# ScalarE takes over the product of the one-hots with the high parts of the gates, one token at a time

## The chip, the core and the metric

The kernel runs on one core of a Trainium2 chip. The metric is the device time of one execution in microseconds (us). TensorE is PE in the profile (PEld its weight loads), VectorE is DVE, ScalarE is ACT, GpSimd is POOL, SyncE is SP.

## The reference, cut to what matters

The program is two transformer blocks over 512 tokens. The part at stake is the product-key expert layer of the first one (`peer_ffn`): 8 heads choose 16 of 128 x 128 experts each, so every token has 128 picks, and each pick is a pair (a, b) of key numbers with a gate.

```python
idx = jnp.take_along_axis(cand_i, best_p, axis=-1)      # a * 128 + b
gate = jax.nn.softmax(best_s, axis=-1)
act = jax.nn.gelu(jnp.einsum('nd,nhkd->nhk', xi, u[idx]), approximate=False)
return jnp.einsum('nhk,nhkd->nd', (gate * act), v[idx])
```

## The kernel before

For 384 of the 512 tokens (`DT`) the kernel computes all 16384 experts densely. For each token it needs a 128 x 128 matrix of gates: entry (b, a) is the sum of the gates of the picks with that pair. This matrix is a product of two one-hot matrices over the 128 picks, which lie on the 128 partitions: `left` has a one where the key equals the pick's a, `right` where it equals the pick's b, and `right` times the gate is the other factor. The gate is split into a high and a low bf16 part, so the product is taken twice and summed in PSUM. The remaining 128 tokens (`ROW_TILE`) take another way: for each of their picks GpSimd gathers one expert row of 4 KB per partition from `u` or `v` (512 KB for one pick of all 128 tokens) into one of four row slots, and VectorE multiplies or adds it (`VectorProgram.rows`).

The stage at stake is `gate_matrices`. It has 48 steps (`HOT_STEPS`) of 8 tokens (`OC`). The one-hots lie as [group of 4 tokens, key, token], so that the four tokens of a group (`OI`) are neighbours in memory, and one token's 128 keys lie 8 bytes apart. In a step of the kernel before:

- **VectorE** writes `left` (L1981), `right` (L1984), `right` times the gates' high parts (L1986) and `right` times the low parts (L1987), each 128 x 1024 bf16. Then it uses the gathered rows that are due, 1.5 per step on average (`ROWS_HOT`; L1827 dots with `u`, L1840 sums with `v`), and, once in 8 steps, in the fourth of them, subtracts the low part of a weight block (L1851, 128 x 4096).
- **TensorE** waits for the step's one-hots, does 16 matmuls of 128 x 128 (L802: 8 tokens, two parts), and after every odd step a *fill tile*: 24 matmuls of 384 columns for one tile of expert activations (`fill`, L456 to L458). In the kernel before, both matmuls of a token load the same `left` as weights and stream one of the gated ones.
- **ScalarE** copies the two PSUM banks of a step into `gate_matrices` (L1348, with a strided write: four tokens go side by side for each key), takes the fill tile through Gelu (L1304), and once in 8 steps, before the Gelu of the second one, writes the high part of a weight block (L1060, 128 x 4096).
- **SyncE** stores 2 MB of gate matrices every 4 steps, loads 2 MB of weights every 8 steps (once the low part that frees the stage buffer is done; its next entries stand behind that wait), and spills each fill tile (192 KB).
- **GpSimd** issues the row gathers, each when the row four before it has been used.

The one-hots are double buffered over steps (`v = n % 2`), except `right`, which has one buffer. VectorE may begin step n when TensorE has done step n-2. All engines run orders written out by hand; semaphores join them, and each engine works strictly down its own list. "A period" below is 8 steps: 4 fill tiles, 12 gathered rows, one weight block, two stores. The stage is 6 periods. It is followed by fill tiles alone (`LAST_FILL`) and then the expert sums, in which TensorE has work without a break.

Of the kernel before, what the change touches and what calls it, by code (L numbers as in the profile page):

```python
# [14 lines left out]
P = 128  # L15
D = 1024
# [60 lines left out]
class Signals:  # L77


    def __init__(self, nc, reached):  # L80
# [51 lines left out]
        self.row_act = self.new("row_experts_activated")  # L132

# [14 lines left out]
        self.hot = self.new("one_hots_ready")  # L148
# [39 lines left out]
class Layout:  # L188


    def __init__(self, nc, n_columns):
# [54 lines left out]
        self.left, self.right = hot("one_hot_a", one_hots, BF16), hot("one_hot_b", one_hots[:1] + one_hots[2:], BF16)  # L246
        self.gated = [hot(f"gated_one_hot_b_{part}", one_hots, BF16) for part in range(2)]
# [13 lines left out]
        self.row_sum = Map(nc, m.at)("row_sum", [P, D])  # L261
# [168 lines left out]
class TensorProgram:  # L430
# [361 lines left out]
    def gate_matrices(self):  # L792
        nc, s, k, m = self.nc, self.s, self.k, self.m
        for n in range(DT // OC):
            v = n % 2
            nc.tensor.wait_ge(*s.hot.at(n))
            for q in range(OC // 4):
                event = ("gate_mats", n, q)
                i = self.take(event, (s.act_out, event))
                for x in range(4):  # L800
                    for part in range(2):
                        ins = nc.tensor.matmul(k.psum[:, i, NK * x:NK * (x + 1)], m.left[:, v, q, :, x],  # L802
                                               m.gated[part][:, v, q, :, x], start=part == 0, stop=part == 1)
                ins.then_inc(*s.gate_mats.up(n, q))
# [241 lines left out]
class ScalarProgram:  # L1046
# [290 lines left out]

    def gate_matrices(self):
        nc, s, k, m = self.nc, self.s, self.k, self.m
        for n in range(HOT_STEPS):  # L1340
# [177 lines left out]
class VectorProgram:  # L1518
# [374 lines left out]
    def route(self):  # L1893
# [5 lines left out]
        for o, t in enumerate(ROUTE_TILES):  # L1899
# [61 lines left out]
            nc.vector.wait_ge(*s.copied.at("picks", t))  # L1961
            nc.vector.tensor_tensor(m.pick_b[:, 3, at], k.psum[:, k.bank_of["picks", t], 2 * P:3 * P],
                                    m.pick_b[:, 2, at], ALU.subtract).then_inc(*s.routed.up("split", t))

    def gate_matrices(self):
# [8 lines left out]
        for n in range(HOT_STEPS):  # L1974
            v, tokens = n % 2, slice(OC * n, OC * (n + 1))
            number_a, number_b, gate_high, gate_low = (
                m.pick_b[:, x, tokens].rearrange("p (c n) -> p c n", n=OI).unsqueeze(2).to_broadcast(hots)
                for x in range(4))
            if n >= 2:
                nc.vector.wait_ge(*s.gate_mats.at(n - 2, OC // 4 - 1))  # L1980
            nc.vector.tensor_tensor(m.left[:, v], iota, number_a, ALU.is_equal).then_inc(*s.step.up())  # L1981
            if n >= 1:
                nc.vector.wait_ge(*s.hot.at(n - 1))
            nc.vector.tensor_tensor(m.right[:, :, :, :], iota, number_b, ALU.is_equal).then_inc(*s.step.up())  # L1984
            nc.vector.wait_ge(*s.step.now())
            nc.vector.tensor_tensor(m.gated[0][:, v], m.right[:, :, :, :], gate_high, ALU.mult).then_inc(*s.step.up())  # L1986
            nc.vector.tensor_tensor(m.gated[1][:, v], m.right[:, :, :, :], gate_low, ALU.mult).then_inc(*s.hot.up(n))  # L1987
# [493 lines left out]
```

## Time and profile before

| | |
|---|---|
| median of 3 runs | 2749.22 us (2747.74 to 2750.6) |
| the profiled execution, its own time | 2750.3 us |
| its span | 2749.0 us |
| busy: PE, DVE, ACT, POOL | 2468.8, 1567.8, 964.3, 889.2 us |
| gate-matrix stage, first one-hot to the Gelu of its last fill tile | 1177.3 to 1435.4 us of the span |

Busy times are sums over the whole span; what a change in one stage is worth has to be read from that stage. The granted TensorE clock is in tenths of full speed: 1.0 is 2.4 GHz, 0.5 is 1.2 GHz. Matmuls overlap, so two starts are nearer than one matmul is long; the same holds to a smaller degree for ScalarE and VectorE.

### The profile page before, as it was taken

How to read it: one execution, taken by the hardware profiler on the slowest of the kernel's cores; microseconds unless marked ns; L12 is line 12 of the kernel's file. 1: busy time of each engine (PE TensorE's matmuls, PEld its weight loads, DVE VectorE, ACT ScalarE, POOL GpSimd, SP SyncE). 2: the span in 40 equal slices, each digit the busy share in tenths (PEclk: the TensorE clock that was granted, in tenths of full speed). 3: DMA queues.
4: the chain of work that ended last, by engine and by line, in shares of the span. 5: the costliest groups of instructions: out<-in, count | busy, mean ns of one | idle time of the engine just before them, and what ended most of it. 6: DMA issues, size and time to landing. Idle time of an engine off the chain costs nothing.

```text
span 2749.0 us, 32835 instructions
## 1 busy us (share of the span) xinstructions
PE 2468.8 (90%) x13363; PEld 1442.8 (52%) x13363; DVE 1567.8 (57%) x2616; ACT 964.3 (35%) x1122; POOL 889.2 (32%) x686
## 2 busy tenths in 40 slices
PE   6997679997879997968789999999979988899998
PEld 4455446653445554555565566666534466344443
DVE  2036452213289999998986888886455375333102
ACT  3116542313233333344444333333242343334310
POOL 3332252432114143334432333331116100354540
PEclk8998766889989999988889999999999998999999
DMA  4121111231159686778899999998412100123310
GB/s 167 62 93 62 63 62 62 92 123 55 54 172 327 231 316 214 280 266 307 297 342 327 382 389 382 385 376 297 153 46 92 51 28 8 62 94 121 123 62 31
DMA packets 194503, 484.78 MB, mean 176 GB/s; under 512 B 10741, under 2 KB 93731, under 8 KB 188336
## 3 DMA queue, kind: packets, MB, share of 16 engines
q1 hardware_dynamic: 154624, 334.65, 34.8%
q0 software_dynamic: 39728, 148.03, 14.3%
q8 instruction: 106, 1.74, 0.3%
q14 instruction: 45, 0.37, 0.0%
HBM read 430.21 MB, written 52.43 MB: 176 GB/s over the span
## 4 chain that ended last, share of the span: by engine, by line
PE 63%; DVE 21%; DMA 7%; ACT 4%; issue 2%; POOL 2%; SPq 0%; ACTq 0%; DVEq 0%; POOLq 0%
PE psum L456 16%; PE psum L457 16%; PE psum L458 16%; DMA rows_b<-u_rows_dram,row_index 4%; DVE weight_low L1851 3%; PE psum L707 3%; POOL weight_low L2153 2%; PE psum L689 2%; PE psum L514 2%; DMA rows_b<-peer_v_dram,row_index 2%; DVE row_sum L1840 1%; PE psum L941 1%; DVE picks L1943 1%; DVE rows_b L1827 1%; PE psum L601 1%
## 5 line engine op out<-in xcount | busy, mean ns | idle before, releaser
L456 PE MATMUL psum<-x_high,weight_high 128*128 128x384 bf16 (+3 forms) x1856 | 652.6, 352 | 67.2 <-DVE weight_low L1851 29.6
L2153 POOL TENSOR_TENSOR weight_low<-weight_stage,weight_high 128x512 bf16<-128x512 f32 (+1 forms) x373 | 463.9, 1281 | 740.7 <-ACT weight_high L1060 740.7
L457 PE MATMUL psum<-x_low,weight_high 128*128 128x384 bf16 (+3 forms) x1856 | 651.8, 351 | 0.0
L458 PE MATMUL psum<-x_high,weight_low 128*128 128x384 bf16 (+3 forms) x1856 | 650.4, 350 | 0.0
L1060 ACT ACTIVATE weight_high<-weight_stage 128x4096 bf16<-128x4096 f32 (+2 forms) x112 | 399.2, 3566 | 343.0 <-PE psum L458 310.4
L456 PE MATMUL psum<-hidden_high,weight_high 128*128 128x384 bf16 x1024 | 333.8, 326 | 1.0 <-DVE hidden_low L2006 0.9
L458 PE MATMUL psum<-hidden_high,weight_low 128*128 128x384 bf16 x1024 | 333.8, 326 | 0.0
L457 PE MATMUL psum<-hidden_low,weight_high 128*128 128x384 bf16 x1024 | 333.8, 326 | 0.0
L456 PEld LDWEIGHTS psum<-x_high,weight_high 128*128 128x128 bf16 (+1 forms) x1856 | 186.2, 100 | 236.9 <-issue 37.3
L1851 DVE TENSOR_TENSOR weight_low<-weight_stage,weight_high 128x4096 bf16<-128x4096 f32 x64 | 282.8, 4419 | 29.0 <-ACT weight_high L1060 29.0
L458 PEld LDWEIGHTS psum<-x_high,weight_low 128*128 128x128 bf16 (+1 forms) x1856 | 186.3, 100 | 159.3 <-issue 14.7
L457 PEld LDWEIGHTS psum<-x_low,weight_high 128*128 128x128 bf16 (+1 forms) x1856 | 186.0, 100 | 149.2 <-issue 10.6
L2256 POOL DMA_INDIRECT rows_a<-u_rows_dram,row_index x64 | 88.7, 1386 | 355.6 <-DVE rows_a L1827 265.7
L1304 ACT ACTIVATE norm_value<-psum 128x384 f32<-128x384 f32 x128 | 62.8, 491 | 354.0 <-PE psum L458 185.7
L2256 POOL DMA_INDIRECT rows_b<-u_rows_dram,row_index x64 | 96.6, 1510 | 218.5 <-DVE rows_b L1827 217.0
L802 PE MATMUL psum<-gated_one_hot_b,one_hot_a 128*128 128x128 bf16 x768 | 97.7, 297 | 52.8 <-DVE gated_one_hot_b L1987 52.7
L2256 POOL DMA_INDIRECT rows_b<-peer_v_dram,row_index x64 | 102.8, 1607 | 117.6 <-DVE row_sum L1840 101.3
L456 PEld LDWEIGHTS psum<-hidden_high,weight_high 128*128 128x128 bf16 x1024 | 100.2, 98 | 67.6 <-issue 1.7
L458 PEld LDWEIGHTS psum<-hidden_high,weight_low 128*128 128x128 bf16 x1024 | 100.2, 98 | 66.2
L457 PEld LDWEIGHTS psum<-hidden_low,weight_high 128*128 128x128 bf16 x1024 | 100.2, 98 | 65.5
L2256 POOL DMA_INDIRECT rows_a<-peer_v_dram,row_index x64 | 96.7, 1510 | 84.1 <-DVE row_sum L1840 64.1
L802 PEld LDWEIGHTS psum<-gated_one_hot_b,one_hot_a 128*128 128x128 bf16 x768 | 85.9, 120 | 65.2 <-DVE gated_one_hot_b L1987 63.1
(321 smaller groups left out, 3551.5 us busy)
## 6 DMA issues: line engine op xcount, KB each, us to landing
weight_stage<-peer_u_dram SPq DMA_DIRECT2D x32, 2048.0 KB
weight_stage<-peer_v_dram SPq DMA_DIRECT2D x32, 2048.0 KB
weight_stage<-mlp_w_dram SPq DMA_DIRECT2D x16, 2048.0 KB
weight_stage<-ada_w_dram SPq DMA_DIRECT2D x12, 2048.0 KB
act_dram<-norm_value SPq DMA_DIRECT2D x128, 192.0 KB
gate_dram<-gate_matrices SPq DMA_DIRECT2D x12, 2048.0 KB, 17.1
gates<-gate_dram SPq DMA_DIRECT2D x32, 768.0 KB, 16.5
expert_act<-act_dram SPq DMA_DIRECT2D x32, 768.0 KB
```

What stands on the lines that cost most here:

```text
L456: self.nc.tensor.matmul(out, left[0], right[0], start=first, stop=False)
L457: self.nc.tensor.matmul(out, left[0], right[1], start=False, stop=False)
L458: return self.nc.tensor.matmul(out, left[1], right[0], start=False, stop=last)
L514: ins = nc.tensor.matmul(k.bank(i, hi - lo), self.m.ones[:, :], buffers.square[:, t % 4, lo:hi], start=t == 0, stop=t == KT - 1, skip_grou ...
L689: ins = nc.tensor.matmul(k.psum[0:JT, j + ni * i // HT, ni * i % HT:ni * i % HT + ni], ka[rows, a, JT * jt:JT * (jt + 1)], qa[rows, a, i0: ...
L707: ins = nc.tensor.matmul(k.psum[:, 6 + half, i0 - HT * half:i0 - HT * half + ni], m.gv[:, jt, P * head:P * (head + 1)], weight[n % 3][:, n ...
L802: ins = nc.tensor.matmul(k.psum[:, i, NK * x:NK * (x + 1)], m.left[:, v, q, :, x], m.gated[part][:, v, q, :, x], start=part == 0, stop=par ...
L1060: nc.scalar.activation(k.block_view(m.w_high, n % SPLITS, n), k.block_view(m.w_stage, n % STAGES, n), ACT.Copy).then_inc(*s.w_high.up(n))
L1304: nc.scalar.activation(m.norm2.value[:, tile % 4, 0:DT], k.tile_bank(event, DT), ACT.Gelu).then_inc(*s.activated.up(*event))
L1851: nc.vector.tensor_tensor(k.block_view(m.w_low, n % SPLITS, n), k.block_view(m.w_stage, n % STAGES, n), k.block_view(m.w_high, n % SPLITS, ...
L2153: ins = nc.gpsimd.tensor_tensor(m.w_low[:, n % SPLITS, at], m.w_stage[:, n % STAGES, at], m.w_high[:, n % SPLITS, at], ALU.subtract)
L2256: nc.gpsimd.indirect_dma_start(m.rows[i % ROW_SLOTS], None, v if layer else u, index).then_inc(*s.in_rows[i % ROW_SLOTS].up(i))
```

## The change

ScalarE multiplies `left` (the one-hots of a, no longer those of b) with the gates' high parts, one instruction per token: 128 partitions x 128 keys, read 8 bytes apart, written as one contiguous row into a new tile `gated_high`, with the token's column of a new f32 tile `gate_high` as the scale (a [128, 1] operand). VectorE keeps three 128 x 1024 operations: `left`, `right`, and `left` times the low parts. `right` gets a second buffer. TensorE now loads the gated one-hots as weights (the high ones contiguous, the low ones strided as before) and streams `right`. In `ScalarProgram.gate_matrices` the products of step n come ahead of the copies of step n-1. In `route`, VectorE copies each tile's gates once more into f32 (3 copies of 128 x 128).

```diff
+        self.hot_gated = self.new("one_hots_gated")
...
-        self.left, self.right = hot("one_hot_a", one_hots, BF16), hot("one_hot_b", one_hots[:1] + one_hots[2:], BF16)
-        self.gated = [hot(f"gated_one_hot_b_{part}", one_hots, BF16) for part in range(2)]
+        self.left, self.right = hot("one_hot_a", one_hots, BF16), hot("one_hot_b", one_hots, BF16)
+        self.gated_high = hot("one_hot_a_gated_high", [P, 2, OC, NK], BF16)
+        self.gated_low = hot("one_hot_a_gated_low", one_hots, BF16)
...
             nc.tensor.wait_ge(*s.hot.at(n))
+            nc.tensor.wait_ge(*s.hot_gated.at(n, OC - 1))
...
-                    for part in range(2):
-                        ins = nc.tensor.matmul(k.psum[:, i, NK * x:NK * (x + 1)], m.left[:, v, q, :, x],
-                                               m.gated[part][:, v, q, :, x], start=part == 0, stop=part == 1)
+                    for part, left in enumerate((m.gated_high[:, v, 4 * q + x, :], m.gated_low[:, v, q, :, x])):
+                        ins = nc.tensor.matmul(k.psum[:, i, NK * x:NK * (x + 1)], left, m.right[:, v, q, :, x],
+                                               start=part == 0, stop=part == 1)
...
+    def gate_hots(self, n):
+        nc.scalar.wait_ge(*s.hot_made.at(n))
+        if n >= 2:
+            nc.scalar.wait_ge(*s.gate_mats.at(n - 2, OC // 4 - 1))
+        for x in range(OC):
+            at = OC * n + x
+            nc.scalar.activation(m.gated_high[:, v, x, :], m.left[:, v, x // OI, :, x % OI], ACT.Copy,
+                                 scale=m.gate_high[:, at:at + 1]).then_inc(*s.hot_gated.up(n, x))
...
-        for n in range(HOT_STEPS):
+        for step in range(HOT_STEPS + 1):
+            if step < HOT_STEPS:
+                self.gate_hots(step)
+            if step == 0:
+                continue
+            n = step - 1
...
+            nc.vector.tensor_copy(m.gate_high[:, at], m.pick_b[:, 2, at]).then_inc(*step.up())
...
             if n >= 2:
                 nc.vector.wait_ge(*s.gate_mats.at(n - 2, OC // 4 - 1))
-            nc.vector.tensor_tensor(m.left[:, v], iota, number_a, ALU.is_equal).then_inc(*s.step.up())
-            if n >= 1:
-                nc.vector.wait_ge(*s.hot.at(n - 1))
-            nc.vector.tensor_tensor(m.right[:, :, :, :], iota, number_b, ALU.is_equal).then_inc(*s.step.up())
-            nc.vector.wait_ge(*s.step.now())
-            nc.vector.tensor_tensor(m.gated[0][:, v], m.right[:, :, :, :], gate_high, ALU.mult).then_inc(*s.step.up())
-            nc.vector.tensor_tensor(m.gated[1][:, v], m.right[:, :, :, :], gate_low, ALU.mult).then_inc(*s.hot.up(n))
+                nc.vector.wait_ge(*s.hot_gated.at(n - 2, OC - 1))
+            nc.vector.tensor_tensor(m.left[:, v], iota, number_a, ALU.is_equal).then_inc(*s.hot_made.up(n))
+            nc.vector.tensor_tensor(m.right[:, v], iota, number_b, ALU.is_equal).then_inc(*s.step.up())
+            nc.vector.wait_ge(*s.hot_made.at(n))
+            nc.vector.tensor_tensor(m.gated_low[:, v], m.left[:, v], gate_low, ALU.mult).then_inc(*s.hot.up(n))
```

ScalarE's list in the middle of the stage before: the copies of two steps stand together (`gate_matrices`), then a fill tile's Gelu (`norm_value`), once in 8 steps with the weight block's high part (`weight_high`) ahead of it.

```order
L1348 ACTIVATE gate_matrices<-psum 128x4x128 x4
L1304 ACTIVATE norm_value<-psum 128x384
L1348 ACTIVATE gate_matrices<-psum 128x4x128 x4
L1060 ACTIVATE weight_high<-weight_stage 128x4096
L1304 ACTIVATE norm_value<-psum 128x384
```

The same list after the change, two steps with a fill tile and a weight block between them; `one_hot_a_gated_high` are the eight products of a step.

```order
L1351 ACTIVATE one_hot_a_gated_high<-one_hot_a,gates_t_high 128x128 x8
L1369 ACTIVATE gate_matrices<-psum 128x4x128 x2
L1064 ACTIVATE weight_high<-weight_stage 128x4096
L1308 ACTIVATE norm_value<-psum 128x384
L1351 ACTIVATE one_hot_a_gated_high<-one_hot_a,gates_t_high 128x128 x8
L1369 ACTIVATE gate_matrices<-psum 128x4x128 x2
L1351 ACTIVATE one_hot_a_gated_high<-one_hot_a,gates_t_high 128x128 x8
L1369 ACTIVATE gate_matrices<-psum 128x4x128 x2
L1308 ACTIVATE norm_value<-psum 128x384
```

The products of step n+2 stand behind the Gelu of the fill tile that follows step n (n odd), and those of step n+3 behind the copies of step n+1.

VectorE's list, one step before, and one after; `rows_a` and `row_sum` are uses of gathered rows, `in_rows_0` and `in_rows_1` the gathers they wait for.

```order
L1827 SCALAR_TENSOR_TENSOR rows_a,modulation_rows<-rows_a,normed_rows 128x1024 [waits in_rows_0]
L1981 TENSOR_TENSOR one_hot_a<-iota_bf_135,picks_t_bf_107 128x1024 [waits gate_matrices_ready]
L1984 TENSOR_TENSOR one_hot_b<-iota_bf_135,picks_t_bf_107 128x1024 [waits one_hots_ready]
L1986 TENSOR_TENSOR gated_one_hot_b_124<-one_hot_b,picks_t_bf_107 128x1024 [waits vector_steps]
L1987 TENSOR_TENSOR gated_one_hot_b_125<-one_hot_b,picks_t_bf_107 128x1024
L1840 SCALAR_TENSOR_TENSOR row_sum<-rows_a,modulation_rows,row_sum 128x1024 [waits rows_used,in_rows_1]
```

```order
L1848 SCALAR_TENSOR_TENSOR rows_a,modulation_rows<-rows_a,normed_rows 128x1024 [waits in_rows_0]
L2004 TENSOR_TENSOR one_hot_a<-iota_bf_136,picks_t_bf_107 128x1024 [waits one_hots_gated,gate_matrices_ready]
L2005 TENSOR_TENSOR one_hot_b<-iota_bf_136,picks_t_bf_107 128x1024
L2007 TENSOR_TENSOR one_hot_a_gated_low<-one_hot_a,picks_t_bf_107 128x1024 [waits one_hots_made]
L1861 SCALAR_TENSOR_TENSOR row_sum<-rows_a,modulation_rows,row_sum 128x1024 [waits rows_used,in_rows_1]
```

One of four 128 x 1024 operations is gone from each step, and the wait of the second product for the one just before it has become a wait for the one two before.

## Rows read from the trace of the kernel before

**Rows 1.** Windows of the stage, one period, and what follows (columns in the first line).
```profile
core 0: us, PE busy (x) PEld busy (x) DVE busy (x) ACT busy (x) POOL busy (x), PEclk, DMA share, GB/s
1281.40:1324.54 43.14, 33.93 (x226) 24.56 (x225) 38.67 (x52) 21.33 (x22) 16.95 (x13) 0.82 0.85 311
1435.00:1500.00 65.00, 64.94 (x400) 38.93 (x399) 38.35 (x37) 27.39 (x26) 13.69 (x11) 1.00 0.91 325
```

**Rows 2.** Waits in 1177 to 1433: who for whom, us in total, times, longest.
```profile
PE psum L802 <- DVE gated_one_hot_b L1987: 52.7, 29, 4.1
DVE rows_b L1827 <- DMA rows_b<-u_rows_dram,row_index: 21.0, 11, 3.9
DVE row_sum L1840 <- DMA rows_b<-peer_v_dram,row_index: 2.6, 5, 0.6
```

**Rows 3.** VectorE's timeline, one step: start us, us, operation.
```profile
1319.59 0.69 DVE L1981 TENSOR_TENSOR one_hot_a<-iota_bf,picks_t_bf 128x1024 bf16<-128x1024 bf16 x1
1320.19 0.69 DVE L1984 TENSOR_TENSOR one_hot_b<-iota_bf,picks_t_bf 128x1024 bf16<-128x1024 bf16 x1
1320.91 0.69 DVE L1986 TENSOR_TENSOR gated_one_hot_b<-one_hot_b,picks_t_bf 128x1024 bf16<-128x1024 bf16 x1
1321.52 0.68 DVE L1987 TENSOR_TENSOR gated_one_hot_b<-one_hot_b,picks_t_bf 128x1024 bf16<-128x1024 bf16 x1
1322.12 1.22 DVE L1827 SCALAR_TENSOR_TENSOR rows_a<-rows_a,normed_rows 128x1024 f32<-128x1024 f32 x1
```

**Rows 4.** Chain of waits, 1281 to 1330: two gathers from issue to landing (start us, us).
```profile
1289.67 13.40 DMA rows_b<-u_rows_dram,row_index
...
1304.85 9.83 DMA rows_b<-u_rows_dram,row_index
```

**Rows 5.** TensorE's timeline at one short pause; [idle before <-releaser] at the end.
```profile
1404.62 2.05 PE L802 MATMUL psum<-gated_one_hot_b,one_hot_a 128*128 128x128 bf16 x16
1407.20 2.06 PE L802 MATMUL psum<-gated_one_hot_b,one_hot_a 128*128 128x128 bf16 x16 [0.53 <-DVE gated_one_hot_b L1987]
1409.08 0.50 PE L456 MATMUL psum<-x_high,weight_high 128*128 128x384 bf16 x1
...
1411.61 0.44 PE L458 MATMUL psum<-x_high,weight_low 128*128 128x384 bf16 x1
1411.89 0.33 PE L456 MATMUL psum<-x_high,weight_high 128*128 128x384 bf16 x1
1412.06 0.33 PE L457 MATMUL psum<-x_low,weight_high 128*128 128x384 bf16 x1
```

**Rows 6.** TensorE's weight loads at full clock: 32 strided ones, one contiguous one.
```profile
1298.55 3.82 PEld L802 LDWEIGHTS psum<-gated_one_hot_b,one_hot_a 128*128 128x128 bf16 x32
...
1302.83 0.10 PEld L456 LDWEIGHTS psum<-x_high,weight_high 128*128 128x128 bf16 x1
```

**Rows 7.** ScalarE's timeline, Gelu, weight block, copies of two steps.
```profile
1363.90 3.95 ACT L1348 ACTIVATE gate_matrices<-psum 128x512 f32<-128x512 f32 x4 [0.45 <-PE psum L802]
...
1435.49 0.49 ACT L1304 ACTIVATE norm_value<-psum 128x384 f32<-128x384 f32 x1 [2.85 <-PE psum L458]
1435.88 3.61 ACT L1060 ACTIVATE weight_high<-weight_stage 128x4096 bf16<-128x4096 f32 x1
```

**Rows 8.** ScalarE's timeline, runs of one form without and with a [128, 1] operand.
```profile
2038.13 1.74 ACT L1109 ACTIVATE norm_square<-na_q 128x256 f32<-128x256 f32 x5
...
2045.31 1.31 ACT L1120 ACTIVATE ctx_high<-norm_value,modulation 128x256 bf16<-128x256 f32 x3 [2.34 <-DVE norm_value L1575]
```

**Rows 9.** Groups by form on ScalarE: busy us, mean ns of one | idle before.
```profile
L1348 ACT ACTIVATE gate_matrices<-psum 128x512 f32<-128x512 f32 x96 | 95.9, 1088 | 66.6 <-PE psum L802 65.6 <-issue 0.9
...
L1320 ACT ACTIVATE scores<-psum 128x512 f32<-128x512 f32 x16 | 9.6, 597 | 22.8 <-PE psum L776 22.8
...
L1120 ACT ACTIVATE ctx_high<-norm_value,modulation 128x256 bf16<-128x256 f32 x8 | 3.8, 504 | 3.8 <-DVE norm_value L1575 3.8
...
L1109 ACT ACTIVATE norm_square<-na_q 128x256 f32<-128x256 f32 x8 | 2.8, 406 | 0.3 <-issue 0.3
```

More of the change, by code:

```diff
@@ L147, in __init__ @@
         self.routed = self.new("experts_chosen")
-        self.hot = self.new("one_hots_ready")
+        self.hot_made, self.hot = self.new("one_hots_made"), self.new("one_hots_ready")
         self.gated = self.new("hidden_gated")
@@ L260, in __init__ @@
             self.mod_rows[:, PICKS * x:PICKS * (x + 1)] for x in range(4))
-        self.row_sum = Map(nc, m.at)("row_sum", [P, D])
+        behind = Map(nc, m.at)
+        self.row_sum, self.gate_high = behind("row_sum", [P, D]), behind("gates_t_high", [P, DT])
         self.keys = m("sub_keys", [P, 2 * PH, NK])
@@ L1336, in route @@
             self.row_experts(ROWS_ROUTE[ROUTE_TILES.index(chosen)])
+    def gate_hots(self, n):
+        nc, s, m = self.nc, self.s, self.m
+        v = n % 2
+        nc.scalar.wait_ge(*s.hot_made.at(n))
[5 more added lines that the diff above has]
+                                 scale=m.gate_high[:, at:at + 1]).then_inc(*s.hot_gated.up(n, x))
     def gate_matrices(self):
         nc, s, k, m = self.nc, self.s, self.k, self.m
-        for n in range(HOT_STEPS):
+        for step in range(HOT_STEPS + 1):
[4 more added lines that the diff above has]
+            n = step - 1
             chunk, part = n // (TC // OC), n % (TC // OC)
@@ L1975, in gate_matrices @@
             v, tokens = n % 2, slice(OC * n, OC * (n + 1))
-            number_a, number_b, gate_high, gate_low = (
+            number_a, number_b, gate_low = (
                 m.pick_b[:, x, tokens].rearrange("p (c n) -> p c n", n=OI).unsqueeze(2).to_broadcast(hots)
-                for x in range(4))
+                for x in (0, 1, 3))
             if n >= 2:
                 nc.vector.wait_ge(*s.gate_mats.at(n - 2, OC // 4 - 1))
-            nc.vector.tensor_tensor(m.left[:, v], iota, number_a, ALU.is_equal).then_inc(*s.step.up())
-            if n >= 1:
-                nc.vector.wait_ge(*s.hot.at(n - 1))
-            nc.vector.tensor_tensor(m.right[:, :, :, :], iota, number_b, ALU.is_equal).then_inc(*s.step.up())
-            nc.vector.wait_ge(*s.step.now())
-            nc.vector.tensor_tensor(m.gated[0][:, v], m.right[:, :, :, :], gate_high, ALU.mult).then_inc(*s.step.up())
-            nc.vector.tensor_tensor(m.gated[1][:, v], m.right[:, :, :, :], gate_low, ALU.mult).then_inc(*s.hot.up(n))
+                nc.vector.wait_ge(*s.hot_gated.at(n - 2, OC - 1))
[3 more added lines that the diff above has]
+            nc.vector.tensor_tensor(m.gated_low[:, v], m.left[:, v], gate_low, ALU.mult).then_inc(*s.hot.up(n))
             self.rows(ROWS_HOT[n])
```

## The prediction

> **What bounds the kernel now.** First the windows. From 1435 us on TensorE works without a break at full clock [rows 1], and the expert sums behind that are its work too, so what the gate-matrix stage gains or loses in its 258.1 us goes whole into the time. In a period of the stage (43.14 us, 8 steps) TensorE is busy 33.93 us at a mean clock of 0.82, ScalarE 21.33, VectorE 38.67 [rows 1]. The waits say who leads: TensorE waits 52.7 us for VectorE's last product, VectorE only for gathered rows, 21.0 + 2.6 us [rows 2], which is 3.9 us a period. So VectorE's list sets the pace, with the gathers as its second term.
>
> **VectorE's share of the change.** One step's four operations take from 1319.59 to 1322.12, 2.53 us, of which 0.72 lie between the second and third start and 0.60 to 0.61 between the others: the third waits for the second [rows 3]. After the change three remain, and the product waits for the operation two before, so 3 x 0.60 = 1.80 us. That is 0.73 less a step, 5.8 us a period. The gathers give part of it back. A slot is refilled when VectorE has used it, and a refill issued into the stores and weight loads takes 13.40 and 9.83 us to land [rows 4], whatever VectorE does meanwhile. Four slots at 1.5 rows a step are 2.7 steps, which cover 2.7 x 0.73 = 1.9 us less than before; two waits a period make 3.9 us. VectorE with its gathers would then need 43.0 - 5.8 + 3.9 = 41.1 us a period (43.0 is 258.1/6). This is the floor that the other engines have to stay under.
>
> **ScalarE's share.** A product of 128 elements with a [128, 1] scale is not in the trace. Its neighbours are there: 256 elements take 406 ns without such an operand and 504 with one [rows 9], and back to back three of the latter end after 1.31 us, so 0.403 us from start to start [rows 8]. Five of the former end after 1.74 us, 0.334 apart. The length part: from 256 to 512 elements of the plain form (406 to about 597 ns by the PSUM copies, [rows 9]) is 0.75 ns an element, from the 1.74 us run's 256 elements to the 4096 of the weight block (3.61 us, [rows 7]) 0.83. With 0.83, half the length takes 0.107 us off: 0.296 us from start to start, 0.40 for one alone. Eight are 2.37 us of ScalarE, and the last one is done 7 x 0.296 + 0.40 + 0.06 = 2.53 us after the first begins. I bound the pitch below by 0.25 (the operand costs nothing in a stream) and above by 0.42: the copies into `gate_matrices` write with a stride and take 1088 ns where contiguous ones take 597 [rows 9], 0.96 ns an element more, and the products read with a stride of 8 bytes. I take 0.296, since all but the stride is measured, and the doubled row has a stride of 128 bytes, on the write side. By the doubled row the sum would be 24 us above mine (the third rival). SBUF — State Buffer in the Trainium skill (the note on 16-byte cachelines) says that a strided read keeps full bandwidth while two accesses fall in one 16-byte line; 8 bytes is just that, and by this rule the stride costs nothing. No row here shows a strided read on ScalarE.
>
> A period's ScalarE work becomes 64 x 0.296 = 18.9 for the products, 16 x 0.95 = 15.2 for the copies (four end after 3.95, [rows 7]), 3.5 for the weight block and 4 x 0.39 for Gelu [rows 7]: 39.2 us where it had 21.3. It now nearly fills the period, and its order matters.
>
> **The new loop.** The products of step n+2 stand behind the Gelu of the fill tile after step n, and that fill tile stands behind the matmuls of step n on TensorE. So from one Gelu to the next, two steps on, one chain runs: Gelu 0.39; eight products 2.53; 16 matmuls; the fill tile; Gelu. The 16 matmuls took 1407.20 to 1409.08, 1.88 us [rows 5]. Their weight loads go at 3.82/32 = 0.119 us strided and 0.10 contiguous [rows 6]; half become contiguous, so 1.88 - 8 x 0.019 = 1.73. The fill tile is 23 x 0.1625 (64.94 us for 400 matmuls, [rows 1]) + 0.37 = 4.11 us at full clock. The clock will not be full. In the loop TensorE finishes the even step's matmuls (their products are ready) and then waits about 1 us for the odd step's, and a pause of only 0.53 us in just this place put the nine matmuls after it on the 1.2 GHz level, 0.32 apart instead of 0.16 [rows 5]. Nine are 1.4 us; I take 1.0, since the phase will vary. Sum: 0.39 + 2.53 + 1.73 + 4.11 + 1.0 = 9.8, times four 39.0.
>
> Once a period the weight block comes in. Then ScalarE, after the odd step's products, still has 1.9 (copies), 2.4 (products), 1.9 (copies), 3.5 = 9.7 us before Gelu, while TensorE needs 0.05 + 1.73 + 4.11 + 1.0 = 6.9: 2.8 us over. Without the block 6.2 is under 6.9. VectorE's low part makes one `left` a period late; I put 0.4 for it, between nothing and 1. A period: 39.0 + 2.8 + 0.4 = 42.2 us, above VectorE's 41.1 and 0.8 below today's 43.0. Six periods: -4.8.
>
> **Small terms.** The first matmul waits for `left` and eight products, 0.69 + 2.53, instead of 2.65: +0.5. Three f32 copies of 128 x 128 in `route`: only the last is ahead of the stage, +0.2. The second `right` buffer changes nothing, as VectorE was never stopped by the first. TensorE's count, DMA bytes and all tables of ScalarE stay. Sum -4.8 + 0.7 = -4.1, so the profiled 2750.3 becomes 2746; against the median (2749.2) that is 3 us less. A measurement of this kernel can tell about 0.2% (5.5 us) from no change, so my likeliest case is no measurable change.
>
> **Rivals.**
> *The loop stays at full clock.* If the shorter, regular pauses leave the clock up, the loop is 8.8 x 4 + 3.8 + 0.4 = 39.4, and VectorE with its gathers decides at 41.1: 6 x 1.9 = -11, 2739. For it: TensorE's idle share falls; against: the 0.53 us pause [rows 5].
> *VectorE's whole gain arrives.* If in addition the gathers land earlier, because the stores follow the copies and shift, the waits stay at 3.9 and the period is the loop's 39.4 or so: -22, 2728. Against: bytes per us rise while the DMA share is already 0.85 [rows 1].
> *ScalarE's products become the bound* (the other side). ScalarE's list is then full. Its pair of steps is 0.39 + 16 p + 3.8 with p the pitch; four of them and the block are 43.0 at p = 0.355, and with the loop's wait for TensorE the turn comes earlier, at about 0.31, only 15 ns above my figure. At 0.35 the period is some 44.5 and the kernel 2759; at 0.42, ScalarE alone needs 26.9 + 20.3 = 47.2 and the kernel is at 2775. For it: the doubled copies [rows 9]; TensorE stands, VectorE idles. ScalarE: Activation LUTs in the Trainium skill (rules for kernel authors) says to multiply on VectorE, not ScalarE. Row by row it would speak for this rival: 8 x 0.296 = 2.37 us replace 0.73. It leaves open that the engine giving is the bound and the one taking idles.
> That the change doesn't do what it says I rule out: the products are in ScalarE's list and gone from VectorE's.
>
> **How the numbers follow.** The loop with clock dips, 0.40 (2740 to 2752; a quarter of it under -5.5); the loop at full clock 0.20; the whole gain 0.10; products moderately dear (pitch 0.32 to 0.36) 0.16; products doubled 0.14. Faster: 0.20 + 0.10 + 0.10 = 0.40. Within 0.2%: 0.28 of the first and a little of the fourth, 0.30. Slower: 0.30. The range leaves out the far parts of the second and last rival: 2728 to 2771.
>
> **What would show it.** Right: the products at 0.40 us alone and 0.29 to 0.30 apart, ScalarE busy over 85% of the stage; TensorE waiting once per two steps, now for ScalarE's products, 0.8 to 1.5 us; a longer such wait once in 8 steps, where the weight block stands; fill tiles still partly on the 1.2 GHz level; VectorE's own four operations down to 1.80 us, and its idle time grown, for rows or for TensorE's step n-2. The step that is weakest is the clock in the loop, then the stride. Wrong: TensorE waiting for VectorE's low product as now (the gathers lead, not the loop), or products over 0.31 apart.

## The result, and the profile after

| | before | after |
|---|---|---|
| median | 2748.11 us (20 runs) | 2754.12 us (20 runs) |
| ratio | | 1.0028 [1.0019, 1.0036] |
| the profiled execution, its own time | 2750.3 us | 2753.76 us |
| its span, mean TensorE clock | 2749.0 us, 0.916 | 2752.5 us, 0.914 |
| stage: first one-hot to the Gelu of its last fill tile | 1177.32 to 1435.49 us | 1178.89 to 1443.27 us |

The changed kernel is slower by 0.28%, 6.0 us by the medians and 7.7 by the ratio. A time of 2746 had been predicted, with no measurable change as the likeliest case. In the profiled runs the stage takes 6.2 us more, close to the 6.0 us of the medians, and its last Gelu comes 7.8 us later; 1.4 us of that offset stand in the trace at 113 us already, far ahead of anything that the change touches. Behind the last Gelu the profiled execution of after is 4.3 us shorter (1309.2 against 1313.5 us), although nothing differs there. In all thirteen traces of this case that part takes 1308.2 to 1313.5 us, and two executions of one kernel (e2) are 3.6 us apart in it. So the stages of two traces can be compared, their whole times only by the medians.

The page of after, busy time by engine over the whole span:

```profile
PE 2477.7 (90%) x13295; PEld 1448.3 (53%) x13363; DVE 1536.9 (56%) x2571; ACT 1071.2 (39%) x1506; POOL 873.2 (32%) x686
```

The stage as one window (columns as in [rows 1]):

```profile
1178.90:1440.00 261.10, 218.27 (x1328) 152.55 (x1329) 201.46 (x260) 234.79 (x511) 87.34 (x72) 0.80 0.85 308
```

VectorE is busy 201 of 261 us, no longer nearly all of the time; ScalarE 235 of 261, 90%. The clock of the stage stays at 0.80. The work has moved as planned. Who waits, in 1177 to 1440 (who for whom, us in total, times, longest), against [rows 2]:

```profile
PE psum L806 <- issue: 44.4, 25, 4.9
ACT norm_value L1308 <- PE psum L461: 21.6, 16, 1.8
DVE one_hot_a L2004 <- PE psum L806: 16.3, 12, 3.0
DVE row_sum L1861 <- DMA rows_b<-peer_v_dram,row_index: 15.6, 6, 3.1
DVE weight_low L1872 <- ACT weight_high L1064: 13.5, 6, 3.2
ACT one_hot_a_gated_high L1351 <- DVE one_hot_a L2004: 5.0, 9, 1.6
DVE rows_b L1848 <- DMA rows_b<-u_rows_dram,row_index: 4.7, 4, 2.4
DVE row_sum L1861 <- DMA rows_a<-peer_v_dram,row_index: 3.0, 2, 2.1
```

TensorE waits 44.4 us, but no longer for VectorE. "issue" names no releaser; the pauses lie where the odd steps' products are missing, and in the kernels below that have a matmul in that pause, the same wait is put down to `one_hot_a_gated_high`. ScalarE waits for TensorE's fill tiles 16 times, and VectorE now waits for TensorE, for ScalarE and for rows. So two engines wait for each other in turn. ScalarE's timeline (start, us, engine, line, operation, form, count, [idle before]) shows one turn of it:

```profile
1303.09 0.49 ACT L1308 ACTIVATE norm_value<-psum 128x384 f32<-128x384 f32 x1 [1.72 <-PE psum L461]
1303.48 2.50 ACT L1351 ACTIVATE one_hot_a_gated_high<-one_hot_a,gates_t_high 128x128 bf16<-128x128 bf16 x8
1305.88 2.02 ACT L1369 ACTIVATE gate_matrices<-psum 128x512 f32<-128x512 f32 x2
1307.69 2.46 ACT L1351 ACTIVATE one_hot_a_gated_high<-one_hot_a,gates_t_high 128x128 bf16<-128x128 bf16 x8
1310.05 1.99 ACT L1369 ACTIVATE gate_matrices<-psum 128x512 f32<-128x512 f32 x2
1313.53 0.49 ACT L1308 ACTIVATE norm_value<-psum 128x384 f32<-128x384 f32 x1 [1.49 <-PE psum L461]
...
1322.23 3.62 ACT L1064 ACTIVATE weight_high<-weight_stage 128x4096 bf16<-128x4096 f32 x1
1325.75 0.47 ACT L1308 ACTIVATE norm_value<-psum 128x384 f32<-128x384 f32 x1
```

and TensorE's timeline shows the other half of the turn; answers to [rows 5]:

```profile
1304.63 0.29 PE L806 MATMUL psum<-one_hot_b,one_hot_a_gated_low 128*128 128x128 bf16 x1
1306.08 0.28 PE L806 MATMUL psum<-one_hot_b,one_hot_a_gated_high 128*128 128x128 bf16 x1 [1.15 <-issue]
1306.17 0.30 PE L806 MATMUL psum<-one_hot_b,one_hot_a_gated_low 128*128 128x128 bf16 x1
...
1307.92 0.50 PE L459 MATMUL psum<-x_high,weight_high 128*128 128x384 bf16 x1
1308.22 0.53 PE L460 MATMUL psum<-x_low,weight_high 128*128 128x384 bf16 x1
...
1311.05 0.33 PE L460 MATMUL psum<-x_low,weight_high 128*128 128x384 bf16 x1
1311.21 0.33 PE L461 MATMUL psum<-x_high,weight_low 128*128 128x384 bf16 x1
```

The even step's matmuls are done, TensorE pauses 1.15 us for the odd step's products, and ten of the fill tile's matmuls start about 0.32 us apart (1.2 GHz) before the rest start 0.16 apart (2.4 GHz). In the stage's 24 fill tiles 218 matmuls start at that wide distance, where it was 111 before. They are called slow matmuls from here on.

From Gelu to Gelu (1303.09 to 1313.53) the turn takes 10.44 us: Gelu 0.39, products until the first matmul behind them 2.60 (1303.48 to 1306.08), 16 matmuls 1.84 (to 1307.92), fill tile to Gelu 5.61. The four turns from 1281.46 to 1325.75 take 11.00, 10.63, 10.44 and, with the weight block, 12.22: a period of 44.3 us, where 42.2 had been predicted and 43.0 was the old one. Of the five whole periods between the Gelus behind a weight block, three are like that (44.25, 44.29, 44.34); the first takes 42.8 and the last 41.4. The stage as a whole takes 264.4 us, a sixth of it 44.1.

### The profile page after: what moved, and what is told of

It reads as the page before. It is cut to its first block, busy times and chain, and to the rows that moved or that the text cites. A ratio compares the mean times of both kernels' runs of the same rounds, so it can differ in the third digit from the quotient of the medians.

```text
span 2752.5 us, 33198 instructions
## 1 busy us (share of the span) xinstructions
PE 2477.7 (90%) x13295; PEld 1448.3 (53%) x13363; DVE 1536.9 (56%) x2571; ACT 1071.2 (39%) x1506; POOL 873.2 (32%) x686
## 4 chain that ended last, share of the span: by engine, by line
PE 70%; DVE 17%; ACT 4%; issue 3%; DMA 3%; POOL 2%; SPq 0%; ACTq 0%; DVEq 0%; POOLq 0%
PE psum L459 17%; PE psum L460 17%; PE psum L461 17%; PE psum L806 3%; PE psum L710 3%; DVE weight_low L1872 3%; POOL weight_low L2173 2%; PE psum L692 2%; PE psum L517 2%; DMA rows_b<-peer_v_dram,row_index 2%; DVE picks L1964 1%; PE psum L945 1%; PE psum L604 1%; ACT weight_high L1064 1%; DVE norm_value L1596 1%
## 5 line engine op out<-in xcount | busy, mean ns | idle before, releaser
L460 PE MATMUL psum<-x_low,weight_high 128*128 128x384 bf16 (+3 forms) x1843 | 654.7, 355 | 21.0 <-DVE x_low L1605 14.8
L459 PEld LDWEIGHTS psum<-x_high,weight_high 128*128 128x128 bf16 (+1 forms) x1856 | 188.0, 101 | 240.5 <-issue 43.6
L806 PE MATMUL psum<-one_hot_b,one_hot_a_gated_high 128*128 128x128 bf16 x384 | 92.3, 295 | 44.4 <-issue 44.4
L1351 ACT ACTIVATE one_hot_a_gated_high<-one_hot_a,gates_t_high 128x128 bf16<-128x128 bf16 x384 | 119.4, 398 | 5.0 <-DVE one_hot_a L2004 5.0
L2276 POOL DMA_INDIRECT rows_a<-peer_v_dram,row_index x64 | 81.4, 1272 | 83.3 <-DVE row_sum L1861 64.6
```

Of the source, the lines that this page charges most:

```text
L459: self.nc.tensor.matmul(out, left[0], right[0], start=first, stop=False)
L460: self.nc.tensor.matmul(out, left[0], right[1], start=False, stop=False)
L806: ins = nc.tensor.matmul(k.psum[:, i, NK * x:NK * (x + 1)], left, m.right[:, v, q, :, x], start=part == 0, stop=part == 1)
L1351: nc.scalar.activation(m.gated_high[:, v, x, :], m.left[:, v, x // OI, :, x % OI], ACT.Copy, scale=m.gate_high[:, at:at + 1]).then_inc(*s. ...
L2276: nc.gpsimd.indirect_dma_start(m.rows[i % ROW_SLOTS], None, v if layer else u, index).then_inc(*s.in_rows[i % ROW_SLOTS].up(i))
```

## Experiments

Theory A: the loop of ScalarE and TensorE sets the period, and its fill tiles run partly at 1.2 GHz because of the pause in the loop itself. The rivals: VectorE or the gathers set the period; the clock does not matter; the products' price matters more than their place. All ratios are to the kernel before on the same chip. The diffs of e4 are against the kernel before, the others against the changed kernel unless said.

### e1: products ahead of the Gelu

```diff
-        for step in range(HOT_STEPS + 1):
-            if step < HOT_STEPS:
-                self.gate_hots(step)
-            if step == 0:
-                continue
-            n = step - 1
+        for n in range(2):
+            self.gate_hots(n)
+        for n in range(HOT_STEPS):
...
+            if n + 2 < HOT_STEPS:
+                self.gate_hots(n + 2)
```

> The changed kernel with one thing moved on ScalarE: the eight products of step n+2 stand right behind the copies of step n, ahead of the weight block and the Gelu of the fill tile, so they no longer wait for the end of that fill tile. ScalarE's work is the same. Theory A (the closed loop Gelu, products, matmuls, fill tile, Gelu sets the period of 44.3 us): the loop is open, the pauses of 1.13 and 3.1 us ahead of the odd steps shrink or go, the period falls to 41 to 42.6 us, where VectorE with its gathers and ScalarE's list meet, and the kernel to 2735 to 2744. Rival B (ScalarE's amount of work is the bound): nothing moves by more than 3 us, about 2754. Rival C (VectorE with the gathers still leads): also about 2754, with VectorE never waiting for TensorE.

Measured: 2749.84 us (12 runs), ratio 1.0009 [1.0000, 1.0019]; about 4 us under the changed kernel. Theory A had promised 2735 to 2744, so it gets the direction and misses the size. Its waits, 1177 to 1440:

```profile
ACT one_hot_a_gated_high L1351 <- DVE one_hot_a L2003: 25.9, 13, 2.9
DVE row_sum L1860 <- DMA rows_b<-peer_v_dram,row_index: 17.6, 6, 4.3
DVE weight_low L1871 <- ACT weight_high L1064: 17.6, 6, 3.7
```

ScalarE hardly waits for the fill tiles any more (2.3 us, once, instead of 21.6), so the loop is open, and the slow matmuls fall from 218 to 78. In its place two waits across VectorE grow: ScalarE's weight block now stands behind one more row of products, VectorE's low part waits longer for it (17.6 us instead of 13.5), and ScalarE's products wait longer for VectorE's one-hots (25.9 us instead of 5.0). VectorE's waits for rows grow too, from 23.3 to 39.7 us. The mean of four periods is 42.6 us (fill tiles from 1254.13 to 1424.63); the same four of the changed kernel take 43.6 (1242.03 to 1416.31). ScalarE's list alone would need 39.2 by the prediction's sum.

### e2: matmuls in the pause

TensorE does 384-column matmuls of no use into the bank that the step writes next, ahead of its wait for the odd step's one-hots: 7, and 20 in the step whose products follow the weight block. They end about where the products do, so they should take no time of their own.

```diff
+            first = self.take(("gate_mats", n, 0), (s.act_out, ("gate_mats", n, 0)))
+            for _ in range(0 if n % 2 == 0 or n < 3 else 20 if n % 8 == 3 else 7):
+                nc.tensor.matmul(k.psum[:, first, 0:DT], m.x_high[:, 0, 0:P], m.x_high[:, 1, 0:DT], start=True, stop=True)
```

> The changed kernel with 7 extra matmuls of 384 columns (20 once in 8 steps, ahead of the step after the weight block) on TensorE in its pause ahead of each odd step's one-hots, into the PSUM bank that the step then overwrites. They only keep TensorE busy while it waits. Theory A with the clock term: the nine or so matmuls a fill tile that run at the 1.2 GHz level (218 in the stage, 0.16 us each) go to full clock, the loop loses about 1.4 us a pair of steps, and the period falls from 44.3 to 41 or 42 us, where VectorE with its gathers takes over: 2735 to 2742. Rival (the clock is a side effect, the period is ScalarE's work or the gathers'): 2752 to 2756, fill tiles at full clock or not.

It was measured a second time, beside e9 and e10:

> The kernel of e2_paused_matmuls once more (7 extra matmuls ahead of odd steps, 20 in the step of the weight block), as the neighbour of the next two on the same chip. Both theories: a ratio to the kernel before of 0.997 to 0.9995, time 2740 to 2745.

Measured: 2742.81 us (12 runs), ratio 0.9984 [0.9975, 0.9993], and the second time 2742.88 us (11 runs), 0.9984 [0.9975, 0.9993]. It is 11 us faster than the changed kernel, by added work alone, and faster than the kernel before; theory A's range ended 0.8 us below it. Slow matmuls: 47 in the first profiled run, 22 in the second, instead of 218. The stage's window has the clock at 0.95:

```profile
1178.90:1440.00 261.10, 247.08 (x1660) 177.12 (x1660) 202.29 (x258) 238.49 (x510) 95.33 (x72) 0.95 0.85 316
```

Its Gelus (ScalarE's timeline) give the turn at full clock:

```profile
1358.37 0.46 ACT L1311 ACTIVATE norm_value<-psum 128x384 f32<-128x384 f32 x1
1368.92 0.49 ACT L1311 ACTIVATE norm_value<-psum 128x384 f32<-128x384 f32 x1 [1.01 <-PE psum L461]
1377.93 0.49 ACT L1311 ACTIVATE norm_value<-psum 128x384 f32<-128x384 f32 x1
1386.95 0.49 ACT L1311 ACTIVATE norm_value<-psum 128x384 f32<-128x384 f32 x1
```

9.01 and 9.02 us; where a pause of 1.16 us was left over, behind the weight block, ten matmuls are slow and the turn takes 10.55. The price of the clock in the loop is thus 1.5 us for ten slow matmuls. Not every turn is that short (the 18 without the weight block take 9.71 us on average): the mean period is 41.6 us (four from 1237.62 to 1404.07), and the waits name VectorE's side:

```profile
DVE row_sum L1864 <- DMA rows_a<-peer_v_dram,row_index: 17.3, 8, 2.8
DVE row_sum L1864 <- DMA rows_b<-peer_v_dram,row_index: 13.4, 6, 2.7
DVE rows_b L1851 <- DMA rows_b<-u_rows_dram,row_index: 8.8, 6, 2.3
ACT one_hot_a_gated_high L1354 <- DVE one_hot_a L2007: 11.1, 12, 2.5
```

With the loop nearly at full clock, the waits for rows rise to 39.5 us, 6.6 a period, from 23.6 [rows 2] and 23.3 in the changed kernel.

### e3: no low product

VectorE's low product is left out, and TensorE takes the plain one-hots in its place, so the output has ones in the place of the gates' low parts.

```diff
-                    for part, left in enumerate((m.gated_high[:, v, 4 * q + x, :], m.gated_low[:, v, q, :, x])):
+                    for part, left in enumerate((m.gated_high[:, v, 4 * q + x, :], m.left[:, v, q, :, x])):
...
-            nc.vector.tensor_tensor(m.gated_low[:, v], m.left[:, v], gate_low, ALU.mult).then_inc(*s.hot.up(n))
```

> The changed kernel without VectorE's product with the low parts: TensorE takes the plain one-hots of a as the second part, so the low parts of the gates are left out of the computation (ones in their place) and VectorE has 0.6 us less in each step. Theory A (the loop over ScalarE and TensorE sets the period, VectorE idles): within 2 us of the changed kernel, 2752 to 2756. Rival C (VectorE with the gathers sets it): up to 8 times 0.6 us a period less, given back in part by the gathers, 2735 to 2745.

Measured: 2753.5 us (10 runs), ratio 1.0024 [1.0014, 1.0035], with 219 slow matmuls. VectorE's 48 x 0.6 us = 29 us of work are gone and the time stays that of the changed kernel. VectorE waits that much more: 36.1 us for TensorE instead of 16.3, 28.1 for rows instead of 23.3, and 17.6 for the weight block instead of 13.5.

```profile
DVE one_hot_a L2004 <- PE psum L806: 36.1, 26, 3.7
```

That rules VectorE's list out as the bound of the changed kernel, as theory A had it (2752 to 2756).

### e4: the same matmuls in the kernel before

```diff
+            first = self.take(("gate_mats", n, 0), (s.act_out, ("gate_mats", n, 0)))
+            for _ in range(0 if n < 3 else 8 if n % 2 else 6):
+                nc.tensor.matmul(k.psum[:, first, 0:DT], m.x_high[:, 0, 0:P], m.x_high[:, 1, 0:DT], start=True, stop=True)
```

> The kernel before with extra matmuls of 384 columns ahead of each step's one-hots (8 ahead of odd, 6 ahead of even steps), in TensorE's pauses. Theory A: before the change VectorE sets the period and TensorE only follows, so a fuller clock brings nothing: 2746 to 2751, while the slow matmuls of the fill tiles (111 in the stage) become fewer. Rival (the 1.2 GHz stretches cost their own time in either kernel): 111 times 0.16 us, up to 15 us less.

Measured: 2748.22 us (12 runs), ratio 1.0005 [0.9994, 1.0017], with 11 slow matmuls in the stage's tiles instead of 111 (window 1177 to 1435):

```profile
1177.00:1435.00 258.00, 241.46 (x1659) 175.95 (x1660) 233.51 (x310) 128.69 (x129) 102.05 (x72) 0.97 0.86 311
```

The clock of the stage goes from 0.82 to 0.97 and the time does not move. Where VectorE leads, TensorE's clock is slack; in the loop of the changed kernel it is on the path. e2 and e4 together show that it is not the clock as such that the change lost by, but that it put the clock on the path.

### e5, e6, e7: the weight block's low part later

In e5 (against e1) VectorE takes the weight block's low part one step later, so that it need not wait for ScalarE. e6 has the same in e2, and e7 adds 6 matmuls ahead of the even steps to e5.

```diff
-    if any(_tile % EG == 0 for _tile in HOT_FILL[max(0, _n - 1)]) and _n > 0:
-        _next = HOT_FILL[_n - 1][0] // EG + 2
+    if _n >= 2 and any(_tile % EG == 0 for _tile in HOT_FILL[_n - 2]):
+        _next = HOT_FILL[_n - 2][0] // EG + 2
```

> Products ahead of weight block and Gelu on ScalarE, as in the run with early products (2749.8 us), and on VectorE the weight block's low part one step later (behind the rows of the fifth step of a period instead of the fourth). In the run before, VectorE waited 17.6 us for the weight block's high part, now behind the products, and ScalarE then 25.9 us for VectorE's next one-hots. Theory A' (opening the loop moved the bound to VectorE's list, through this wait and the gathers): the wait falls under 5 us, some 2 us a period go, and the kernel comes to 2736 to 2743. Rival (the gathers alone fill the gap): they take up what the wait leaves, and it stays within 3 us of 2750.

> The changed kernel with the extra matmuls in TensorE's pauses (2742.8 us) and the weight block's low part one step later on VectorE. If VectorE's wait for the high part (12.6 us, of which one is 9.2) still cost anything there: 2 to 6 us less, 2737 to 2741. If the loop at full clock or the gathers set the period: no change, 2741 to 2745.

> Early products, late low part, and 6 extra matmuls ahead of each even step, where TensorE paused 1.4 to 2.1 us in the run with early products (78 slow matmuls in the stage). Theory A' says TensorE follows VectorE there, as in the kernel before, so a fuller clock brings nothing: within 3 us of the same kernel without the extra matmuls. If the clock counts here too: 5 to 12 us less.

| | median | ratio | slow matmuls |
|---|---|---|---|
| e5 | 2744.89 us (11 runs) | 0.9988 [0.9977, 1.0000] | 81 |
| e6 | 2747.34 us (11 runs) | 0.9999 [0.9990, 1.0008] | 29 |
| e7 | 2750.84 us (11 runs) | 1.0012 [1.0003, 1.0021] | 82 |

e5 gives 5 us over e1, which is between its two expectations (2736 to 2743, and within 3 us of 2750): the wait for the weight block shrinks by 12.6 us, but one for rows grows by 14.2 (`row_sum`, 17.6 us in e1).

```profile
DVE row_sum L1860 <- DMA rows_b<-peer_v_dram,row_index: 31.8, 6, 6.9
DVE weight_low L1871 <- ACT weight_high L1064: 5.0, 3, 4.3
```

e6 is 4.5 us slower than e2 and e7 6 us slower than e5, which no theory expected. In e6 the longest wait for rows is 5.3 us where it is 2.8 in e2. That the late low part also delays SyncE's next weight load, and so shifts its burst against the gathers, would fit both; it was not tried apart and stays open. e7 says nothing on the clock, because the slow matmuls do not become fewer. Its matmuls stand ahead of even steps, and they shorten the pause there, while the pause just ahead of the slow tiles' own steps, which are odd ones, stays as it was in e5 (2.08 to 2.15 us, 2.13 to 2.17 in e5).

### e8: the price of a product

The scale is the constant 0.5 instead of the gate, so the output has 0.5 in the place of the gates' high parts.

```diff
-                                 scale=m.gate_high[:, at:at + 1]).then_inc(*s.hot_gated.up(n, x))
+                                 scale=0.5).then_inc(*s.hot_gated.up(n, x))
```

> The changed kernel with a constant 0.5 as the scale of ScalarE's products in place of the token's column of gates; so the high parts of the gates are left out of the computation. It measures the price of the [128, 1] operand and the slope of the loop. The product should take about 0.30 us instead of 0.395 and start every 0.205 to 0.21 us instead of 0.30. Theory A (one step's eight products lie in the loop of two steps, so 0.75 us a pair, 3 us a period, until VectorE with its gathers takes over at about 41 to 42): 2736 to 2743. If ScalarE's total work were the bound, 16 products a pair would count, 6 us a period, 2720 to 2728. If the operand costs nothing in a stream: no change.

Measured: 2738.6 us (5 runs), ratio 0.9963 [0.9949, 0.9976], as theory A had it. The profiled execution is the longest of the five (2749.09 us): its stage starts 5.9 us later than that of the changed kernel and takes 249.6 us, 14.8 less, so the stage itself shows what the median shows. In the stage of the changed kernel and of e8:

```profile
L1351 ACT ACTIVATE one_hot_a_gated_high<-one_hot_a,gates_t_high 128x128 bf16<-128x128 bf16 x384 | 119.4, 398 | 5.0 <-DVE one_hot_a L2004 5.0
```

```profile
L1351 ACT ACTIVATE one_hot_a_gated_high<-one_hot_a 128x128 bf16<-128x128 bf16 x384 | 84.5, 307 | 36.1 <-DVE one_hot_a L2004 36.1
```

The [128, 1] operand costs 91 ns an instruction. Eight plain ones end after 1.73 to 1.79 us, 0.205 us apart. That takes 0.7 us out of each turn; ScalarE now waits 36.1 us for VectorE's one-hots instead of 5.0, and VectorE with its gathers sets the period, 41.3 us (four from 1233.39 to 1398.46), though 147 matmuls are still slow.

### e9 and e10: more and fewer matmuls in the pause

Both against e2: 27 instead of 20 in the weight block's step (e9); 4 and 16 instead of 7 and 20 (e10).

```diff
-            for _ in range(0 if n % 2 == 0 or n < 3 else 20 if n % 8 == 3 else 7):
+            for _ in range(0 if n % 2 == 0 or n < 3 else 27 if n % 8 == 3 else 7):
```

> e2 with 27 instead of 20 extra matmuls in the one step of a period with the weight block. In e2 a pause of 1.16 to 1.18 us is left there and the fill tile behind it has 10 or 11 matmuls on the 1.2 GHz level (5.77 us instead of 4.09). Theory A (the clock in ScalarE's loop is what the change lost by): these tiles become 4.09 us, slow matmuls in the stage's tiles under 20 instead of 47, the pair of steps after the block falls from 10.6 to 9.0 us from Gelu to Gelu. VectorE with its gathers needs about 41 us a period and e2 is at 41.6, so no more than 6 x 0.6 = 3.6 us come through: 0.5 to 3.5 us under e2. Rival B (VectorE's list and the gathers already decide every period of e2): slow matmuls fall all the same, but the time stays within 1 us of e2's, and ScalarE's wait for VectorE's one-hots grows by what the loop gains (11.1 us to 17 or more).

> e2 with 4 and 16 extra matmuls in place of 7 and 20, so that a pause of about 0.6 us is left ahead of each odd step instead of 0.05, and of about 1.8 instead of 1.2 in the step of the weight block. Theory A, first form (any pause of half a microsecond in this place lowers the clock, as the 0.53 us pause of the kernel before did): 8 to 11 matmuls of each fill tile at 1.2 GHz, 170 to 220 in all, a period of 43.5 to 44.3, time 2750 to 2755, as if no extra matmul were there. Second form (the clock goes by how long the pause is): half as many, 90 to 140, a period near 43, time 2745 to 2750.

e9: 2743.89 us (11 runs), ratio 0.9990 [0.9979, 1.0001], 9 slow matmuls. The clock is all but full, and the time is 1.0 us above that of e2 measured beside it, about where rival B had it and not where theory A did (0.5 to 3.5 us below). The period is that of e2 as well, 41.6 us (four from 1239.98 to 1406.25), which speaks for VectorE with its gathers as the bound from e2 on. It is not settled: the stage of the profiled execution takes 250.0 us where it is 251.8 and 252.7 in the two traces of e2, the intervals of the two ratios overlap, and ScalarE's wait for VectorE (9.8 us) did not grow as B wanted, nor did the waits for rows (39.6 us).

e10: 2745.18 us (11 runs), ratio 0.9987 [0.9977, 0.9997], 50 slow matmuls. Neither form expected so few; the time is at the lower end of the second form's. Sixteen tiles have a pause of 0.2 to 1.0 us just ahead of their step, and none of them has a slow matmul; of the seven pauses of 1.17 to 1.90 us after the first tile, six have 3 to 11 slow matmuls behind them and one (1.33 us) has none:

```profile
1334.81 0.28 PE L809 MATMUL psum<-one_hot_b,one_hot_a_gated_high 128*128 128x128 bf16 x1 [0.97 <-ACT one_hot_a_gated_high L1354]
...
1337.17 0.33 PE L459 MATMUL psum<-x_high,weight_high 128*128 128x384 bf16 x1
1337.34 0.33 PE L460 MATMUL psum<-x_low,weight_high 128*128 128x384 bf16 x1
...
1343.81 0.28 PE L809 MATMUL psum<-one_hot_b,one_hot_a_gated_high 128*128 128x128 bf16 x1 [0.53 <-ACT one_hot_a_gated_high L1354]
```

In the changed kernel each pause of 1.10 to 1.21 us had 5 to 11 slow matmuls behind it. So little was missing to a full clock: 4 matmuls a pause brought most turns back to it. With 218, 50, 47, 22 and 9 slow matmuls (the changed kernel, e10, the two traces of e2, e9) the stage takes 264.4, 252.0, 251.8, 252.7 and 250.0 us.

## Why the prediction was wrong

**What bounds the kernel now: right.** VectorE led before: e4 gives TensorE its clock back and gains nothing.

**VectorE's share: right.** Three starts 0.60 apart, 1.81 us a step against 1.80 predicted:

```profile
1304.96 0.69 DVE L2004 TENSOR_TENSOR one_hot_a<-iota_bf,picks_t_bf 128x1024 bf16<-128x1024 bf16 x1 [0.35 <-PE psum L806]
1305.57 0.68 DVE L2005 TENSOR_TENSOR one_hot_b<-iota_bf,picks_t_bf 128x1024 bf16<-128x1024 bf16 x1
1306.17 0.69 DVE L2007 TENSOR_TENSOR one_hot_a_gated_low<-one_hot_a,picks_t_bf 128x1024 bf16<-128x1024 bf16 x1
```

The floor under it, 41.1 us a period with 7.8 us of waits for rows, is seen where the loop is out of the way: 41.3 in e8, 41.6 in e2 and e9, with 7.0 us of such waits in e8 and 6.6 in e2.

**ScalarE's share: right.** Eight products end after 2.46 to 2.50 us, 0.30 apart and 0.395 alone, against 0.296 and 0.40. The stride of 8 bytes costs nothing, as SBUF — State Buffer in the Trainium skill (the note on 16-byte cachelines) has it; this trace agrees. The third rival, with dearer products, falls. ScalarE: Activation LUTs in the Trainium skill (rules for kernel authors) says to multiply on VectorE; the outcome agrees, but not by the price of the product, which was as forecast.

**The new loop: here it failed, by size.** The loop, its place, its pause (1.10 to 1.21 us, predicted about 1) and the once longer one (2.98 to 3.18) are as described. But the sum of a turn was too small:

| per turn or period, us | predicted | measured |
|---|---|---|
| turn at full clock | 8.76 | 9.02 (e2) |
| in it: products to the first matmul | 2.53 | 2.65 (e2), 2.60 |
| in it: 16 matmuls | 1.73 | 1.86 (e2), 1.84 |
| in it: fill tile to Gelu | 4.11 | 4.12 (e2) |
| the clock | 1.0 | 1.41 |
| turn without the weight block | 9.76 | 10.43, mean of 18 |
| turn with it | 12.56 | 12.22, mean of 5 |
| a late low part, per period | 0.4 | 0.41 to 0.45, off the chain |

The measured clock term is the mean turn less that of e2 at full clock; 0.05 us of e2's turn may belong to the added matmuls, whose last one ends 0.1 us after the products. The late low part makes ScalarE wait 0.41 to 0.45 us for `left` once a period, but for products that TensorE needs only after the fill tile, so no turn is longer for it. That it is the clock shows inside the changed kernel too, in the one period that ran fast:

```profile
1370.09 0.48 ACT L1308 ACTIVATE norm_value<-psum 128x384 f32<-128x384 f32 x1
1379.50 0.53 ACT L1308 ACTIVATE norm_value<-psum 128x384 f32<-128x384 f32 x1
1389.31 0.49 ACT L1308 ACTIVATE norm_value<-psum 128x384 f32<-128x384 f32 x1 [0.89 <-PE psum L461]
1399.30 0.49 ACT L1308 ACTIVATE norm_value<-psum 128x384 f32<-128x384 f32 x1 [0.50 <-PE psum L461]
```

Its three turns of 9.41, 9.81 and 9.99 us have 3, 5 and 7 slow matmuls; those of 10.44, 10.63 and 11.00 us above have 10, 11 and 13. All six lie within 0.1 us of 9.02 + 0.15 for each slow matmul.

The pause of 0.53 us in [rows 5] had cost 1.4 us, "nine are 1.4 us", and the prediction took 1.0 of it "since the phase will vary". That is the step that failed. The number of slow matmuls a tile did vary, from 3 to 14, but around nine, and not below it as the discount had it: the mean over the turns was the full 1.41. The pause came back in every turn, at nearly the same length. Over the 18 turns without the block that is 18 x 0.41 = 7.4 us, and the turn at full clock is another 18 x 0.26 = 4.7. Against it stand 5 x 0.34 = 1.7 from the turns with the block and 5 x 0.4 = 2.0 for the late low part. The turn with the weight block owes nothing to the clock: it goes by ScalarE's list, and takes 12.2 to 12.3 us here and 12.3 to 12.4 in e2 and e9, where the clock is all but full. That makes 8.4 of the 10.3 us between the stage's forecast (-4.1) and its result (+6.2); 1.8 lie ahead of the first Gelu and were not taken apart. Either of the two errors alone would have left the forecast near no change; the clock alone turns its sign (-4.1 + 7.4).

Of the 0.26 us, 0.11 to 0.13 came from reading [rows 6] too far and 0.07 to 0.12 from the time from the first product to the first matmul. The 0.10 us of contiguous loads there belongs to streams of 384 columns. Between matmuls of 128 columns both kinds take the same (TensorE's weight loads in the stage, count, busy and mean ns):

```profile
L806 PEld LDWEIGHTS psum<-one_hot_b,one_hot_a_gated_low 128*128 128x128 bf16 x384 | 45.4, 118 | 1.6
L806 PEld LDWEIGHTS psum<-one_hot_b,one_hot_a_gated_high 128*128 128x128 bf16 x384 | 44.6, 116 | 53.0 <-issue 51.1
```

**The rivals.** "The loop stays at full clock" (2739) is what e2 makes of the kernel, 2743. The loop would need 3 x 9.02 + 12.3 = 39.4 us a period there, as forecast, and VectorE with its gathers takes 41.6 instead of 41.1. "The whole gain arrives" did not come in any kernel. The slower side had only dear products as its mechanism; a loop slower than the old period through the clock, the term that the prediction itself called its weakest, should have been a rival with a price: 1.4 us instead of 1.0 in the three turns that it lengthens gives 42.2 + 1.2 = 43.4 us, 6 x 0.4 + 0.7 = 3.1 us slower, half of the stage's 6.2; the other half is the turn at full clock. One figure of the third rival does not fit its own sum: 2775 is 29 us above 2746, and not 24.

**Small terms.** The third f32 copy (`gates_t_high`) takes 0.23 us; the stage's start is 1.6 us later, 1.4 of which are not of the change. No run tells these apart.

## What to carry to other kernels

Work that is moved off the leading engine has to be laid out as the chain it joins: when the receiving engine's list ties its products to a result of the consumer, the turn of that loop is the new floor, however idle the engine looked. Price each pause of the loop with the clock that follows it in every turn, without a discount for good phases, and compare the margin with the range of that one term. If a short pause on TensorE is on the path, matmuls of no use in it can be worth more than the work moved: here 0.9984 against 1.0028.

## What was not expected of the hardware

- The length of a pause alone does not tell TensorE's clock behind it. Behind the pause of 1.15 us shown above ten matmuls ran at 1.2 GHz, and behind 0.97 and 0.53 us in e10 none. But behind 0.98 us in e8, where no matmuls were added, nine did, and behind the 0.53 us of [rows 5] nine did too. What else decides was not measured. The pause in e8, with one of the slow matmuls behind it:

```profile
1293.03 0.28 PE L806 MATMUL psum<-one_hot_b,one_hot_a_gated_high 128*128 128x128 bf16 x1 [0.98 <-issue]
1295.50 0.53 PE L461 MATMUL psum<-x_high,weight_low 128*128 128x384 bf16 x1
1295.82 0.53 PE L459 MATMUL psum<-x_high,weight_high 128*128 128x384 bf16 x1
```

- Added TensorE work paid: 239 extra matmuls, in a stage whose mean clock rose from 0.80 to 0.95 with them, made the kernel 11 us faster (e2), and 316 in the kernel before cost and gained nothing (e4).
- A contiguous layout of the weights gained nothing measurable: 116 against 118 ns a load.
